# A two-block transformer forward pass: the middle of its first block rearranged on all engines

## The reference

```python
mh = head_layernorm(mlstm(silu(conv(p["m_q"])), silu(conv(p["m_k"])), p["m_v"], i_pre, f_pre))
ya = sigmoid(p["m_o"]) * mh * silu(p["m_z"])                  # 1024 wide, 4 heads of 256
kc = gelu(blocks(p["n_kc"]) @ w1_k) @ w2_k                    # compression: 31 blocks of 32 tokens
vc = gelu(blocks(p["n_vc"]) @ w1_v) @ w2_v
ks, kw = rope(p["n_ks"]), rope(p["n_kw"])                     # rotations of keys, and of the queries q
o_c = softmax(q kc^T / 8, masked) vc                          # compressed branch
o_s = softmax(rope(q) ks^T / 8, causal) vs                    # all blocks are selected (8 of 8 at 512 tokens)
o_w = softmax(rope(q) kw^T / 8, causal) vw                    # the window (512) covers all tokens
yb = (g0*o_c + g1*o_s + g2*o_w) * silu(p["n_z"])              # 512 wide, 8 heads of 64
x = x + (sigmoid(p["g_a"]) * (ya @ w_branch_a) + sigmoid(p["g_b"]) * (yb @ w_branch_b)) @ w_out
```

## Time and profile before

| | us |
|---|---|
| median of 3 runs | 2188.54 |
| lowest, highest | 2186.83, 2190.27 |
| the profiled execution's own time | 2190.45 |
| its span, first to last instruction | 2188.8 |

### The profile page before, as it was taken

The page is one execution under the profiler, slowest core; times in us unless marked ns, Lnnn a source line. Parts: engine busy times, 40 slices in busy tenths (PEclk is TensorE's granted clock), DMA queues, the critical chain, the costliest instruction groups (busy, mean ns, idle before and its releaser), DMA issues.

```text
span 2188.8 us, 26092 instructions
## 1 busy us (share of the span) xinstructions
PE 2042.5 (93%) x9478; PEld 1661.5 (76%) x9478; DVE 1008.9 (46%) x1464; ACT 819.9 (37%) x1358; POOL 170.1 (8%) x193
## 2 busy tenths in 40 slices
PE   6999876689989999999999998999989999999998
PEld 5888655566668887788888777788868877888886
DVE  6687434444434333533333375955454334333332
ACT  4342331344543233443432265433343324343332
POOL 1102002000000002000001111004300010000010
PEclk9999987589999999999999999999999999999999
DMA  8868305011103333233332322221223432333321
GB/s 286 262 177 289 108 1 118 21 41 35 39 3 99 98 99 87 77 96 96 96 99 87 114 75 71 81 71 42 58 68 89 136 97 77 97 94 102 99 86 59
DMA packets 336376, 209.63 MB, mean 96 GB/s; under 512 B 21225, under 2 KB 323238, under 8 KB 336038
## 3 DMA queue, kind: packets, MB, share of 16 engines
q1 hardware_dynamic: 325072, 170.58, 27.6%
q0 software_dynamic: 10368, 37.75, 4.9%
q10 hardware_dynamic: 854, 0.20, 0.0%
HBM read 203.26 MB, written 5.24 MB: 95 GB/s over the span
## 4 chain that ended last, share of the span: by engine, by line
PE 79%; DVE 10%; ACT 4%; DMA 3%; issue 2%; ACTq 1%; POOL 0%; DVEq 0%; SPq 0%; POOLq 0%
PE psum L425 22%; PE psum L427 21%; PE psum L426 21%; DVE delta_qkv_T L1896 2%; PE psum L1065 2%; DMA ada_w<-in_ada_w 2%; PE psum L1266 1%; PE psum L1084 1%; PE psum L1016 1%; PE psum L967 1%; PE psum L982 1%; DVE w_lo L384 1%; DVE ada_sum L1896 1%; PE psum L1074 1%; PE psum L878 1%
## 5 line engine op out<-in xcount | busy, mean ns | idle before, releaser
L425 PE MATMUL psum<-act_hi,w_hi 128*128 128x512 f32 x1616 | 649.6, 402 | 17.8 <-DVE w_lo L384 7.0
L427 PE MATMUL psum<-act_hi,w_lo 128*128 128x512 f32 x1616 | 637.0, 394 | 0.0
L426 PE MATMUL psum<-act_lo,w_hi 128*128 128x512 f32 x1616 | 636.9, 394 | 0.0
L384 DVE TENSOR_TENSOR w_lo<-w_raw,w_hi 128x1024 fp32r<-128x1024 f32 x306 | 386.1, 1266 | 376.3 <-ACT w_hi L376 354.4
L425 PEld LDWEIGHTS psum<-act_hi,w_hi 128*128 128x128 f32 x1616 | 307.7, 190 | 110.1 <-issue 42.6
L376 ACT ACTIVATE w_hi<-w_raw 128x1024 fp32r<-128x1024 f32 x306 | 319.7, 1052 | 172.2 <-PE psum L427 155.8
L427 PEld LDWEIGHTS psum<-act_hi,w_lo 128*128 128x128 f32 x1616 | 307.6, 190 | 66.5
L426 PEld LDWEIGHTS psum<-act_lo,w_hi 128*128 128x128 f32 x1616 | 308.2, 191 | 61.6 <-issue 0.5
L703 POOL TENSOR_TENSOR squares<-squares 128x512 f32<-128x512 f32 x30 | 46.2, 1549 | 1414.4 <-ACT squares L1453 911.6
L425 PE MATMUL psum<-ffn_hi,w_hi 128*128 128x512 f32 x352 | 139.6, 396 | 0.0
L427 PE MATMUL psum<-ffn_hi,w_lo 128*128 128x512 f32 x352 | 139.0, 395 | 0.0
(11 more groups left out here) (350 smaller groups left out, 2519.3 us busy)
## 6 DMA issues: line engine op xcount, KB each, us to landing
w_raw<-in_ffn_w_in SPq DMA_DIRECT2D x88, 512.0 KB, 3.8
ada_w<-in_ada_w POOLq DMA_DIRECT2D x72, 512.0 KB, 5.7
w_raw<-in_w_in SPq DMA_DIRECT2D x68, 512.0 KB, 3.9
w_raw<-in_mix_w_in SPq DMA_DIRECT2D x52, 512.0 KB, 3.8
w_raw<-in_ffn_w_out SPq DMA_DIRECT2D x32, 512.0 KB, 3.7
w_raw<-in_ffn_w_out SPq DMA_DIRECT2D x16, 384.0 KB, 3.2
w_raw<-in_w_branch_a SPq DMA_DIRECT2D x8, 512.0 KB, 3.6
w_raw<-in_w_out SPq DMA_DIRECT2D x8, 512.0 KB, 3.6
```

Of the source, the lines that this page charges most:

```text
L384: dve.tensor_tensor(WLO[:, n % 4, :], RAW[:, n % 4, :], WHI[:, n % 4, :].bitcast(F32), ALU.subtract).then_inc(w_lo, 1)
L425: pe.matmul(out, whi, hhi, start=start, stop=False)
L426: pe.matmul(out, whi, hlo, start=False, stop=False)
L427: return pe.matmul(out, wlo, hhi, start=False, stop=stop)
```

## The change

The same values are computed. What changes is where work stands on each engine:

- Gate rows: their ACT and DVE steps stand in stage nsa1, a step behind each tile; m goes to DRAM (`m_away`) and comes back as a broadcast over the partitions, which takes the place of `spread_m`. To make room the residual is written to DRAM (`x_away`) in conv1 and read back before out1.
- Gate tiles: `gate_tile(w)` no longer multiplies by h. ACT takes tanh(x/2) in place of the sigmoid (the factor 1/4 or 1/2 is put into later products), DVE makes the product of the two gates, kept in `OG` (all 8 at once). h comes in later with `ya`. So tiles 0 to 6 can be done in the recurrence.
- Recurrence: 20 steps t in place of 4 heads. Step t on PE: score tile t, one quarter, at six steps a rotation matmul, values of tile t-4. Rotations, their angles and the statistics go along in the same steps on DVE, POOL and ACT.
- Compression: `W1` is loaded in natural rows (row 2k and 2k+1 of a block on 128 partitions), both halves before they are used, 16 matmuls each in place of 32; `BLK` takes 8 smaller DVE instructions per half in place of 4. The square root is done by POOL (pow), no longer by ACT.
- Quarters: 8, then 20 in the recurrence, 8 around compression and transposes of h, 12 around the compressed branch, 32 in units 0 to 31 (80 in all, those of nz1 among them); none in units 32 to 63.
- Units: three score banks, turn(u-2) and apply_v(u-3); the maximum is taken as a minimum of negated values, so the negation goes; banks for the values alternate.
- merge1: its first two tiles and the branch-a tile run ahead of the transposes of the result (`y_back`) and of `yb`.

```diff
+        PV_BANK = (7, 4)
+        SCORE_BANK, NSA_PV_BANK, SIDE_BANK, SIDE_FROM = (4, 5, 3), (7, 0), (1, 2), 12
+        ROPED_AT = {5: 4, 7: 5, 9: 0, 11: 1, 13: 2, 15: 3}
+            def load_compress(k):
+                if k == 13:
+                    sp.wait_ge(sem("s_ready"), len(ITEMS))
+                    for s, w1 in enumerate((cmp_w1_k, cmp_w1_v)):
+                        sp.dma_start(W1[:, s], w1[0].rearrange("(k p) h -> p k h", p=P)).then_inc(w1_loaded, 16)
...
+                if name == "out1":
+                    sp.wait_ge(u_lo, UNITS["nz1"])
+                    sp.dma_start(XT[:].rearrange("p k t -> p (k t)"), x_away).then_inc(sem("x_moved"), 16)
...
-            spread_m(0)
-            for h in range(MH):
-                for j in range(NT):
...
+            for t in range(20):
+                if t < 16:
+                    item("s", t)
+                oz(1)
+                if t in ROPED_AT:
+                    item("rope", ROPED_AT[t])
+                if t >= 4:
+                    values(t - 4)
+            oz(2)
...
+            for s in range(2):
+                pe.wait_ge(w1_loaded, 16 + 32)
+                pe.wait_ge(sem("cmp_blocks"), s + 1)
+                for k in range(CB // 2):
+                    mm = pe.matmul(PS[:, (7, 4)[s], 0:62], W1[:, s, k, :], BLK[s][:, k].rearrange("p g n -> p (g n)"),
+                                   start=(k == 0), stop=(k == CB // 2 - 1))
+                mm.then_inc(sem("cmp_hid_sum"), 1)
+            oz(2)
...
-            for u in range(len(units) + 2):
+            for u in range(len(units) + 3):
                 if u < len(units):
                     score(u)
-                if 8 <= u < 56:
-                    oz(u + 8)
-                elif 56 <= u < 64:
-                    quarter(Place("nz1", 0), (u - 56) // 4, u % 4)
-                if 1 <= u <= len(units):
-                    turn(u - 1)
-                if u >= 2:
-                    apply_v(u - 2)
+                if u < 32:
+                    oz(1)
+                if 2 <= u < len(units) + 2:
+                    turn(u - 2)
+                if u >= 3:
+                    apply_v(u - 3)
...
+            def gate_tile(w):      # on ACT
+                pl = Place("oz1", 0)
+                if w < 18:
+                    split_hi(act, pl, w + 4)
...
+                if w % 2 == 0:
+                    if f == 4:
+                        act.wait_ge(sem("decay_ready"), 16)
+                    act.activation(OG[:, f, :], PS[:, bank, :], ACT.Tanh, scale=0.5).then_inc(free, 1)
+                else:
+                    if f:
+                        act.wait_ge(sem("og_ready"), f)
+                    act.activation(ZG[:], PS[:, bank, :], ACT.Tanh, scale=0.5).then_inc(nonlin, 1)
...
+            for t in range(20):      # on DVE
+                h, j = t // 4, t % 4
+                if h in (2, 3) and j == 0:
+                    masked_m(h)
+                if t < 16:
+                    probs(t)
+                rope_angles(t)
+                if t in ROPED_AT:
+                    rope(ROPED_AT[t])
+                if t >= 4:
+                    n = t - 4
+                    if j == 0:
+                        gate_tile(1 + h)
+                    dve.wait_ge(sem("pv_used"), n + 1)
+                    chained(dve.bn_stats(col(BST + 6 * j, 6), MTOK[:, n // 4, j, :]))
+                    cnt.mark(dve.bn_aggr(col(MVS + 2 * n, 2), col(BST + 6 * j, 6)))
+                if t == 17:
+                    blocks(0)
+            blocks(1)
```

More of the change, by code:

```diff
@@ new lines, in values @@
+            def values(t):
+                h, i = t // 4, t % 4
+                if t == 0:
+                    pe.wait_ge(sem("v_ones"), 1)
+                    pe.wait_ge(sem("mod_taken"), 1)
+                    pe.wait_ge(sem("packed_cols"), 1)
+                if t >= 2:
+                    pe.wait_ge(sem("pv_used"), t - 1)
+                pe.wait_ge(sem("p_ready"), ITEMS.index(("s", t)) + 1)
+                for j in range(i + 1):
+                    o = (0, 512, 896, 1152)[j] + (i - j) * P
+                    mm = pe.matmul(PS[:, PV_BANK[t % 2], 0:MD + 1], DP[:, h % 2, o:o + P],
+                                   VTOK[:, j, h, :], start=(j == 0), stop=(j == i))
+                mm.then_inc(sem("pv_ready"), 1)
@@ new lines, in _ @@
+            gate_tile(6)
+            act.wait_ge(sem("cmp_blocks"), 2)
+            for s in range(2):
+                act.wait_ge(sem("k_swap_sum"), s + 1)
+                copy(KVR[:, s, :], PS[:, 5 + s, :]).then_inc(sem("k_swapped"), 1)
+            act.wait_ge(sem("hid_zero"), 3)
+            for s in range(2):
+                act.wait_ge(sem("cmp_hid_sum"), s + 1)
+                for q in ((0, 2), range(4))[s]:
+                    o = NC * (q // 2)
+                    e = act.activation(HID[:, s, q, 0:NC], PS[:, (7, 4)[s], o:o + NC], ACT.Gelu_apprx_tanh)
+                e.then_inc(sem("hid_ready"), 1)
@@ new lines, in _, with yb @@
+                if u in YA_AT:
+                    ya(YA_AT[u])
+                if u >= 7 and (u - 7) % 4 == 0:
+                    add_branch((u - 7) // 4)
+            add_branch(15)
+            for bank in bank_free:
+                dve.sem_inc(bank, (16 + 4 - SIDE_FROM) // 4)
+            def yb():
+                for f in range(4):
+                    dve.wait_ge(sem("yt_ready"), f + 1)
+                    s = NZG[:, f, :]
+                    stt(s, s, 0.5, YT[:, f, :], ALU.mult, ALU.mult).then_inc(product, 1)
+                for f in range(4):
+                    unit_lo(Place("nz1", 0), "nz1", 4, f, YBLO[:, f, :], NZG[:, f, :], YBHI[:, f, :])
```

820 lines of the change are left out of this document (427 added, 393 removed).

## The result

| | before | after |
|---|---|---|
| median, us | 2189.39 | 2137.45 |
| lowest, highest of 4 runs | 2186.83, 2190.27 | 2136.01, 2143.96 |
| ratio | | 0.977, 95% interval 0.9758 to 0.9782 |
| profiled execution's own time | 2190.45 | 2143.96 |
| its span | 2188.8 | 2142.3 |

The changed kernel is 52 us faster. The forecast was 2092 us with a range of 2064 to 2134; the time lies 45 us above the forecast and outside the range.

A forecast was written before the change was run, and what follows sets the result against it. TensorE, busy 93% of the span, was taken as the bound: 273.6 us of work, 34 of waits and 9.8 in merge1 make 317.4 where 414.4 stood, 97.0 less. Forecast 2092 us, range 2064 to 2134.

The forecast's parts named there:

- Rival 1: Blocks 2 and 3: units without a quarter let the clock fall, 69 us less about 3, giving 2158 us; chance 0.09.
- The rule named beside rival 1: Units' three PSUM score banks in turn: short idling between groups makes the clock swing; it would stand behind Rival 1.
- rival 3: Recurrence: clock stays at 1.2 GHz because steps end in short waits; 2332 us, or 2212 at half; chance 0.03.
- rival 2: Units and recurrence: ACT and DVE chains set the steps, +18 us at gate tiles, +12 in recurrence, 2122; chance 0.14.
- The rule of the drain: Four remaining ACT table switches: a drain of about 1380 ns each would add 5.5 us, forecast 2098 instead of 2092.

## Why the prediction was wrong, point by point

Each step against the profiled execution of the changed kernel:

| step | forecast, us | measured | off |
|---|---|---|---|
| gate rows in nsa1 and the start, to the recurrence | 1 | 5.5 (253.20 to 258.74) | +4.5 |
| recurrence | 72.0 + 6 | 68.7 | -9.3 |
| compression, transposes of h | 25.7 + 9 | 26.5 | -8.2 |
| compressed branch | 25.3 + 8 | 34.2 | +0.9 |
| units 0 to 31 | 81.9 + 10 | 86.1 | -5.9 |
| units 32 to 63 | 68.6 | 133.9 | +65.3 |
| merge1's first matmul at | 561 | 608.08 | +47 |
| low clock left over from the units, in merge1 | 0 | 2.5 (18.95 us at 0.87) | +2.5 |
| transposes and `yb`, with the clock behind them | 9.8 | 6.2, and 1.8 of clock (633.26 to 645 us at 0.85) | -1.8 |

**The step that failed** is "There a unit's path from a score's end to its copied probabilities is ... 2.3 us with the hops, against 2.42 of work on TensorE per unit ... I count none", for blocks 2 and 3. The prices of the work were right: 1.87 and 2.42 us per unit were forecast, 1.93 and 2.48 measured as soon as the wait was gone. But the text says itself that one gate tile stands in these blocks, and it counted nothing for it. It stands in unit 32, just where the quarters that had covered its fellows end, and the path has one unit of time, 1.6 to 1.9 us there, and not the two that the third bank seemed to allow. The wait that comes of it is 1.43 us. The other 64 us are the clock behind it, which the sum put at nothing: it took all work in these blocks at full clock. The prediction's own rows had such a case, the second half of the compression, 13.91 us of matmuls of 62 columns at the low clock behind a wait of 10.37. Its first sign of being wrong, a clock below 0.9 in blocks 2 and 3, is the one that came.

**Rival 1** gave the right stretch, the right level (0.50) and the right price (66 us, measured 65), and had 0.09. Its mechanism was wrong: not the lack of a quarter lets the clock fall, since the same list without quarters runs at 1.00 once the wait of 1.43 us is gone from it. Its argument against itself, "at 1.2 GHz it would be busy all the time", is what happened, and was no argument: busy at the low clock is a state that lasts. With the mechanism seen as one wait among narrow work, the chance would have hung on whether the last gate tile is covered, and that can be read from the order.

**The rule named beside rival 1** (the Trainium skill, TensorE: Matmul & The Clock Gate, A second HAM failure mode: psum-queue depth-cycling) is not what acted. Three score banks went round in every kernel here but before, and in the one without the wait the clock was 1.00 for 71 us. The Trainium skill, TensorE: Matmul & The Clock Gate, What's actually happening, says that the default is the throttled clock and that activity releases it. The trace agrees for wide matmuls (1.65 us to 0.91 behind six of them) and disagrees with the plain reading of it for narrow ones: 126.62 us with TensorE busy 125.87 did not release it.

**The recurrence** had one wait, of 1.1 us, and the clock at 1.00: nothing of rival 3, and of rival 2 only 3.4 us of waits in units 0 to 31, in four places, below the 9 of the forecast. TensorE's work in it was 67.5 us, so the sum of single prices (72.0) was 4.5 too high.

**Table loads.** None stands among the units now, as the order said. The rule of the drain made a difference of 6 us, which the parts' errors of 5 to 9 us cover, so the time doesn't tell. The rows show no such gap: the load at 335.87 us starts 0.01 us behind the copy ahead of it on ACT, takes 1.28, and the next activation starts 0.01 us behind it.

**Compression and h.** Both halves took 7.25 us, as priced, the wait for weights of 10.37 is gone, and the waits at the copies of h were 1.9 us, not 5.

**nsa1.** I gave 1 us, between 0 and 4, for its gate rows; it was 5.5 to the recurrence, and the changed kernel is the earliest of nine that are the same up to there, by up to 4.5 us. I had set the DMA of the m rows and of the residual at 0, in a stage whose DVE row shows a wait for its own loads. That row was the warning.

**Behind out1** nothing came back: the first weight load of `ffn_hi` in ffn1_out stands at 1124.1 us in before and 1074.6 in after, 49.5 earlier, and the last one of the program 46.6 earlier, a pace that differs by 3 us over 1050.

## What to carry to other kernels

Narrow matmuls in a row kept the clock they started with here: 1.00 for 71 us, 0.50 for 126. So before wide filler is taken away from such a stretch, look for the last wait in front of it and for any step on another engine that the filler still covered: there a wait of 1.4 us cost 64. Such work should be entered behind wide matmuls and without a gap; where a gap can't be helped, a few redundant wide matmuls behind it can be a cheap repair (with six that brought the clock back, 2.93 us, and 30 more that weren't needed, the kernel was 41 us faster, in one run). Don't count on a wait being short enough: the same wait let the clock fall in one kernel and not in another. And where a profile shows an engine 99% busy, read the granted clock beside it before believing that it is the work that takes the time.

## What the hardware showed that I had not expected

- TensorE at 1.2 GHz, busy 125.87 of 126.62 us, for the whole length of the narrow work. The mean clock over the span, 0.950 to 0.953 in all four executions of the changed kernel (0.979 to 0.984 with gate tile 19 deferred), speaks for its being so in each.
- The work is the same at either level but for the time: a unit of block 2 took 3.58 us at 0.50 and 1.93 at 1.00, one of block 3 4.65 and 2.48.
- The length of a wait alone doesn't decide: one of 1.75 to 1.78 us, at the same instruction, let the clock fall in four kernels and left it at 1.00 in six. 1.21 us left it at 1.00 in the one execution that had it among the units; 1.13 us in the compressed branch was followed by the low clock in twelve kernels of thirteen.
- Adding 48 wide matmuls whose results nobody uses made the kernel 34 us faster.
